# Working two weight chunks together in an fp32r matmul pipeline: all 512-column matmuls of both, then all 256-column matmuls of both

## What is computed

```python
for i in range(DEPTH):
    xn = rms_norm(h, norm_mix[i])
    mix = hgrn2_mixer(xn, ...) if i % 2 == 0 else short_conv_mixer(xn, ...)
    h = h + mix
    h = h + conv_glu_ffn(rms_norm(h, norm_ffn[i]), ffn_w_up[i], ffn_conv[i], ffn_w_down[i])
return rms_norm(h, final_norm)

# inside hgrn2_mixer
q, fr, v, g = jnp.split(xn @ w_in, ...)
f = lb + (1 - lb) * sigmoid(fr);  k = 1 - f
S_t = diag(f_t) S_{t-1} + k_t v_t^T;  o_t = S_t^T q_t      # per head
o = rms_norm(o, out_gain) * silu(g);  return o @ w_out
```

## Time and profile before

| | |
|---|---|
| median of 3 runs | 2368.76 us (2368.31 to 2370.46) |
| the profiled execution | 2369.03 us, of which the span of its instructions is 2367.2 us |
| PE busy | 2339.4 us, 99% |
| DVE busy | 1708.5 us, 72% |
| ACT busy | 1043.5 us, 44% |
| mean DMA rate | 184 GB/s |
| granted TensorE clock | 0.998 of full speed on average |

### The profile page before, as it was taken

One profiled execution on the slowest core, in us unless ns is written; L12 is line 12 of the kernel. 1 busy time (PEld: TensorE's weight loads), 2 busy tenths in 40 slices (PEclk: granted clock), 3 DMA queues, 4 the chain that ended last, 5 costly groups with the idle time before them and its releaser, 6 DMA issues.

```text
span 2367.2 us, 36548 instructions
## 1 busy us (share of the span) xinstructions
PE 2339.4 (99%) x13219; PEld 2049.0 (87%) x13219; DVE 1708.5 (72%) x2153; ACT 1043.5 (44%) x1151; POOL 2.7 (0%) x8
## 2 busy tenths in 40 slices
PE   7999999999999999999999999999999999999998
PEld 6888888888888888888888888888888888888886
DVE  6878788878878878865555666667788788785443
ACT  6443434454444444444444444444444444443443
POOL 0000000000000000000000000000000000000000
PEclk9999999999999999999999999999999999999999
DMA  6555555466666665655556656556656666665664
GB/s 197 169 179 160 166 160 164 152 192 188 186 194 185 187 194 179 194 190 187 188 185 192 188 187 187 187 188 186 194 180 192 189 184 188 193 202 185 193 193 144
DMA packets 411833, 434.90 MB, mean 184 GB/s; under 512 B 13344, under 2 KB 387040, under 8 KB 411616
## 3 DMA queue, kind: packets, MB, share of 16 engines
q1 hardware_dynamic: 411264, 432.51, 59.2%
q10 hardware_dynamic: 480, 1.18, 0.1%
HBM read 431.54 MB, written 2.10 MB: 183 GB/s over the span
## 4 chain that ended last, share of the span: by engine, by line
PE 96%; DVE 1%; issue 1%; ACT 1%; DMA 0%; SPq 0%; ACTq 0%; DVEq 0%
PE acc L1050 54%; PE acc L1056 28%; PE acc L1085 3%; PE acc L1086 3%; PE acc L1084 3%; PE acc L1068 2%; PE side L1179 1%; PE acc L1070 1%; PE side L1151 0%; DMA raw<-in_hgrn_w_in 0%; PE side L1174 0%; ACT w_parts L336 0%; DVE kl L788 0%; DVE a_diag L825 0%; DVE a_diag L819 0%
## 5 line engine op out<-in xcount | busy, mean ns | idle before, releaser
L545 DVE TENSOR_TENSOR w_parts<-raw,w_parts 128x1024 fp32r<-128x1024 f32 x816 | 994.4, 1223 | 578.9 <-ACT w_parts L336 569.0
L336 ACT ACTIVATE w_parts<-raw 128x1024 fp32r<-128x1024 f32 x816 | 862.6, 1060 | 1181.4 <-PE acc L1056 975.4
L1050 PE MATMUL acc<-xn,w_parts 128*128 128x512 f32 x4352 | 1094.5, 393 | 3.2 <-DVE xn L604 3.2
L1050 PEld LDWEIGHTS acc<-xn,w_parts 128*128 128x128 f32 x4352 | 783.7, 189 | 144.3 <-DVE xn L604 3.6
L1056 PEld LDWEIGHTS acc<-xn,w_parts 128*128 128x128 f32 x4352 | 594.1, 190 | 42.8
L1056 PE MATMUL acc<-xn,w_parts 128*128 128x256 f32 x4352 | 607.0, 282 | 0.0
L1050 PE MATMUL acc<-act,w_parts 128*128 128x512 f32 x1216 | 305.0, 393 | 1.6 <-DVE act L859 1.6
L1050 PEld LDWEIGHTS acc<-act,w_parts 128*128 128x128 f32 x1216 | 218.7, 189 | 41.0 <-DVE act L859 1.8
L1056 PEld LDWEIGHTS acc<-act,w_parts 128*128 128x128 f32 x1216 | 165.9, 190 | 11.9
L1056 PE MATMUL acc<-act,w_parts 128*128 128x256 f32 x1216 | 169.5, 282 | 0.0
L1084 PE MATMUL acc<-w_parts,act 128*128 128x512 f32 x352 | 137.3, 390 | 0.0
(11 more groups left out here) (131 smaller groups left out, 1005.2 us busy)
## 6 DMA issues: line engine op xcount, KB each, us to landing
raw<-in_ffn_w_up SPq DMA_DIRECT2D x352, 512.0 KB, 4.1
raw<-in_ffn_w_down SPq DMA_DIRECT2D x176, 512.0 KB, 4.3
raw<-in_hgrn_w_in SPq DMA_DIRECT2D x128, 512.0 KB, 3.6
raw<-in_sc_w_in SPq DMA_DIRECT2D x96, 512.0 KB, 4.5
raw<-in_hgrn_w_out SPq DMA_DIRECT2D x32, 512.0 KB, 3.6
raw<-in_sc_w_out SPq DMA_DIRECT2D x32, 512.0 KB, 4.6
x_tok<-in_x SPq DMA_DIRECT2D x4, 512.0 KB, 8.0
out<-h SPq DMA_DIRECT2D x4, 512.0 KB, 4.1
```

The source lines that it names most:

```text
L336: nc.scalar.activation(w_parts[:, c % RING, :, 0, :], raw[:, c % RING], ACT.Copy).then_inc(hi_ready, 1)
L545: v.tensor_tensor(w_parts[:, c % RING, :, 1, :], raw[:, c % RING], w_parts[:, c % RING, :, 0, :].bitcast(F32), ALU.subtract).then_inc(lo_r ...
L1050: mm(to[:, j, :], w[:, q, 0, j * P:(j + 1) * P], src[:, k * KW + q, :, :].rearrange("p n t -> p (n t)"), start=begin and q == 0, stop=Fals ...
```

## The change

The chunks are taken in pairs everywhere but in DOWN1. For a pair (k0, k0+1) TensorE does the 512-column matmuls of both chunks, then the `pieces` of chunk k0 (stages included), then the 256-column matmuls of both, then the pieces of k0+1. In the value group the 512-column matmuls read high and low weights (`token_boths`), the 256-column ones the high weights (`token_highs`). `chunk_used` is split in two semaphores: `hi_used` frees the high slot for ScalarE, `lo_used` the low slot for VectorE. For a feature chunk `hi_used` comes after its 512-column matmuls and `lo_used` after its 256-column ones; in the value group it is the other way round. In `PLAN`, level 0 moves from n = 3 to 4, level 2 from 6 to 7.

```diff
+RUN = 2
...
 LEVEL, OUTPUT = range(2)
-PLAN = [(2, LEVEL, -1), (3, LEVEL, 0), (5, LEVEL, 1), (6, LEVEL, 2), (8, LEVEL, 3), (10, LEVEL, 4),
+PLAN = [(2, LEVEL, -1), (4, LEVEL, 0), (5, LEVEL, 1), (7, LEVEL, 2), (8, LEVEL, 3), (10, LEVEL, 4),
         (12, LEVEL, 5), (13, LEVEL, 6), (15, LEVEL, 7), (18, OUTPUT, 0)]
...
-                act_e.wait_ge(chunk_used, at(i, phase.cpi, c + 1))
+                act_e.wait_ge(hi_used, at(i, phase.cpi, c + 1))
                 nc.scalar.activation(w_parts[:, c % RING, :, 0, :], raw[:, c % RING], ACT.Copy).then_inc(hi_ready, 1)
 
             def correction(i, phase, g, part, c):
 
-                act_e.wait_ge(chunk_used, at(i, phase.cpi, c + 1 + RING))
+                done = hi_used if phase is HGRN_IN and g == V_GROUP else lo_used
+                act_e.wait_ge(done, at(i, phase.cpi, c + 1 + RING))
                 a = g * phase.parts + part
                 act_e.wait_ge(acc_free, at(i, phase.api, phase.a0 + a + SETS))
...
                 dve.wait_ge(hi_ready, at(i, phase.cpi, c + 1))
+                dve.wait_ge(lo_used, at(i, phase.cpi, c + 1))
                 v.tensor_tensor(w_parts[:, c % RING, :, 1, :], raw[:, c % RING],
                                 w_parts[:, c % RING, :, 0, :].bitcast(F32), ALU.subtract).then_inc(lo_ready, 1)
...
-                        dve.wait_ge(chunk_used, at(i, phase.cpi, c + 1 + RING))
+                        dve.wait_ge(lo_used, at(i, phase.cpi, c + 1 + RING))
...
                 stage(s, [lambda to, j=j: mm(to[:, 0:T], ones[:], sq_acc[:, j, :], start=(j == 0), stop=(j == 1))
                           for j in range(2)] + (token_sums(T) if tokens_too else []))
 
-            def features(to, c, src, k, begin, end, await_low):
+            def feature_highs(to, c, src, k, begin):
 
                 w = w_parts[:, c % RING]
                 for q in range(KW):
                     for j in range(TW):
-
-                        mm(to[:, j, :], w[:, q, 0, j * P:(j + 1) * P],
-                           src[:, k * KW + q, :, :].rearrange("p n t -> p (n t)"), start=begin and q == 0, stop=False,
-                           skip_group_check=True)
-                await_low()
+                        o = mm(to[:, j, :], w[:, q, 0, j * P:(j + 1) * P],
+                               src[:, k * KW + q, :, :].rearrange("p n t -> p (n t)"), start=begin and q == 0,
+                               stop=False, skip_group_check=True)
+                o.then_inc(hi_used, 1)
+
+            def feature_lows(to, c, src, k, end):
+
+                w = w_parts[:, c % RING]
                 for q in range(KW):
                     for j in range(TW):
                         o = mm(to[:, j, T:], w[:, q, 1, j * P:(j + 1) * P], src[:, k * KW + q, 0, :], start=False,
                                stop=end and q == KW - 1, skip_group_check=True)
-                return o
-
-            def tokens(to, c, src, k, begin, end, await_low):
+                o.then_inc(lo_used, 1)
+
+            def x_block(src, t, n, b):
+
...
                 w = w_parts[:, c % RING]
-                await_low()
                 for q in range(KW):
-                    t = k * KW + q
                     for b in range(T // P):
-                        x_hi, x_lo = ((x_mirror[:, t, n] if b else src[:, t, n, 0:P]) for n in range(2))
-                        mm(to[:, b, :], x_hi, w[:, q].rearrange("p n d -> p (n d)"), start=begin and q == 0, stop=False,
-                           skip_group_check=True)
-                        o = mm(to[:, b, T:], x_lo, w[:, q, 0, :], start=False, stop=end and q == KW - 1,
-                               skip_group_check=True)
-                return o
-
-            def wide_tokens(to, c, src, k, begin, end, await_low):
+                        o = mm(to[:, b, :], x_block(src, k * KW + q, 0, b), w[:, q].rearrange("p n d -> p (n d)"),
+                               start=begin and q == 0, stop=False, skip_group_check=True)
+                o.then_inc(lo_used, 1)
+
+            def token_highs(to, c, src, k, end):
 
                 w = w_parts[:, c % RING]
-                await_low()
+                for q in range(KW):
+                    for b in range(T // P):
...
-                        o = mm(bank, x_lo, hi, start=False, stop=end and q == KC - 1)
-                return o
+                        low = mm(bank, x_hi, lo, start=False, stop=False)
+                        high = mm(bank, x_lo, hi, start=False, stop=end and q == KC - 1)
+                low.then_inc(lo_used, 1)
+                high.then_inc(hi_used, 1)
 
             def phase_of(phase, src, ready, ready0, per=1, rs=None, pieces=None, carry=None, rs_at=(0, RS_AT)):
+
+                def between(i, first, g, kk):
+                    if carry and first:
+                        carry(g, kk)
+                    if first and rs and (g, kk) == rs_at:
+                        sum_squares(*rs)
+                    if pieces:
+                        pieces(i, first, g, kk)
...
-                            pe.wait_ge(hi_ready, at(i, phase.cpi, c + 1))
-                            work = features
-                            if first and phase is HGRN_IN and g == V_GROUP and part == 0:
-                                pe.wait_ge(mirror_ready, k + 1)
+                        steps = phase.steps(first, g)
+                        run = 1 if phase is DOWN1 else RUN
+                        for k0 in range(0, phase.cpg, run):
+                            chunks = []
+                            for kk in range(k0, k0 + run):
+                                part, k, begin, end = steps[kk]
+                                c = phase.c0 + g * phase.cpg + kk
+                                a = g * phase.parts + part
+                                if begin:
+
+                                    pe.wait_ge(acc_free, at(i, phase.api, phase.a0 + a + 1))
+                                need = k + 1 if phase.parts == 2 else k * KC // TG + 1
+                                if first and g == 0 and need > seen:
+                                    pe.wait_ge(ready, ready0 + need * per)
+                                    seen = need
+                                pe.wait_ge(hi_ready, at(i, phase.cpi, c + 1))
+                                to = acc[:, a % SETS]
+                                if phase is DOWN1:
+                                    pe.wait_ge(lo_ready, at(i, phase.cpi, c + 1 + RING))
+                                    wide_tokens(to, c, src, k, begin, end)
+                                elif phase is HGRN_IN and g == V_GROUP:
+                                    if first and part == 0:
+                                        pe.wait_ge(mirror_ready, k + 1)
+                                    pe.wait_ge(lo_ready, at(i, phase.cpi, c + 1 + RING))
+                                    token_boths(to, c, src, k, begin)
+                                else:
+                                    feature_highs(to, c, src, k, begin)
+                                chunks.append((c, to, k, end))
                             if phase is DOWN1:
-                                work = wide_tokens
-                            elif phase is HGRN_IN and g == V_GROUP:
-                                work = tokens
-                            work(acc[:, a % SETS], c, src, k, begin, end, await_low).then_inc(chunk_used, 1)
-                            if carry and first:
-                                carry(g, kk)
-                            if first and rs and (g, kk) == rs_at:
-                                sum_squares(*rs)
-                            if pieces:
-                                pieces(i, first, g, kk)
+                                between(i, first, g, k0)
+                                continue
+                            for kk in range(k0, k0 + run - 1):
+                                between(i, first, g, kk)
+                            for c, to, k, end in chunks:
+                                if phase is HGRN_IN and g == V_GROUP:
+                                    token_highs(to, c, src, k, end)
+                                else:
+                                    pe.wait_ge(lo_ready, at(i, phase.cpi, c + 1 + RING))
+                                    feature_lows(to, c, src, k, end)
+                            between(i, first, g, k0 + run - 1)
                 loop(pe, phase, body)
 
-            pe.sem_inc(chunk_used, RING)
+            pe.sem_inc(hi_used, RING)
```

More of the change, by code:

```diff
@@ L207, in trunk @@
         lo_ready = sem("lo_ready")
-        chunk_used = sem("chunk_used")
+        hi_used = sem("hi_used")
+        lo_used = sem("lo_used")
         acc_free = sem("acc_free")
@@ L475, in final @@
                 if first and (g, kk) == (0, 0):
-                    act_e.wait_ge(chunk_used, DOWN1.c0 + RING)
+                    act_e.wait_ge(lo_used, DOWN1.c0 + RING)
```

(40 more changed lines are left out.)

7 lines of the change are left out of this document (added).

## The result

| | before | after |
|---|---|---|
| median of 4 runs beside each other | 2369.59 us (2368.31 to 2370.46) | 2385.99 us (2385.4 to 2388.3) |
| ratio, with its 95% interval | | 1.007 (1.0057 to 1.0082) |
| span of the profiled execution | 2367.2 us | 2383.6 us |
| granted clock, mean | 0.998 | 0.994 |

The change costs 16.4 us, in the median and in the span alike. The forecast was +8.7 with its top at 2386: the direction is right, the size is about half of what came.

What follows compares the result with a forecast made beforehand. TensorE, busy 99% of the span, was taken as the bound, so any new wait is paid in full. Terms -7.3 + 10.0 + 4.2 + 1.8 = +8.7 on 2369.03 gave 2378 us; own range 2373.5 to 2383, full range 2366 to 2386.

Steps and rivals of the forecast that it cites:

- Change 1: Feature and value-group pairs: one switch per pair instead of per chunk saves 0.020 us in each of 364 pairs, -7.3 us.
- Change 2: HGRN_IN level stages: TensorE waits 2.1 us at stage 1 and 0.9 us over stages 3 to 6, +10.0 us.
- Change 3: Start of HGRN_OUT: last activation tiles come 3.3 us later and more work stands behind them, +4.2 us.
- Change 4: Start-up: activation times stay, but 4.7 us of work instead of 3.0 stands behind the wait ending at 29.16, +1.8 us.
- waits smaller: Rival: VectorE gets through n = 2 and 3 faster, level stages cost what they do now, 2367.7 us; chance 0.18.
- faster: Rival: each saved switch is worth more, 2360 us at 0.07 a pair, or the waits are away, 2361; chance 0.14.
- No saving per pair: Rival: the switch's cost grows with the run, or the skill's rule holds, 2385 us; chance 0.10.
- More waits: Rival: levels 3 and 4 also wait between a pair's runs, 1 us more in each iteration, 2382 us; chance 0.08.

Runs made afterwards that it cites:

- the version with the longer wait: Three unused VectorE multiplications added ahead of level 1's operands in each iteration, against the kernel before, without pairs: 2385.17 us, ratio 1.0063.
- another version, with the same waits: The changed kernel with HGRN_OUT alone put back to chunk by chunk: 2379.0 us, ratio 1.004 against the kernel before.

## Why the prediction was right and where it was wrong

**Change 1 (-7.3) was right.** 0.020 us a pair in 284 pairs measured by themselves, and the whole of it is seen in the version that has pairs only there. The formula of the Trainium skill (TensorE: Matmul & The Clock Gate, section "Back-to-back issue gap"), which the page calls that of isolated matmuls, has no term for what came before, so by it the pairs would gain nothing. The measured 2.779, 2.7835 and 2.793 us a chunk with quads, pairs and single chunks decide against it.

**Change 2 (+10.0) was right in its waits and lacked a term.** In the third iteration, where the clock stayed, everything stands where the working put it. Times after P0 = 281.92: level 1's stage begins at +21.56 (forecast 21.5), after 2.0 us (2.1); the later stages come 1.2 us later than without waits (0.9), of which 0.9 are idle time in the timeline. VectorE's rows, beside the earlier trace rows:

```profile
295.17 1.23 DVE L549 TENSOR_TENSOR w_parts<-raw,w_parts 128x1024 fp32r<-128x1024 f32 x1 [3.58 <-ACT w_parts L338]
298.14 1.21 DVE L549 TENSOR_TENSOR w_parts<-raw,w_parts 128x1024 fp32r<-128x1024 f32 x1
301.27 0.68 DVE L809 TENSOR_TENSOR fpre<-fpre 128x512 f32<-128x512 f32 x1
302.60 0.76 DVE L792 TENSOR_TENSOR kl<-kh,suf 128x256 f32<-128x256 f32 x2
```

The split of n = 2 starts at +13.25 (forecast 13.25), that of n = 3 at +16.22 (16.21), the operands end at +21.44 (21.4). The iteration is 2.44 us longer; forecast were 2.5 of waits less 0.3 of pairs. The other three iterations pay 1.6 us more each for a granted clock of 0.5. This is the step that failed: the working took a wait to cost its own length and 0.1 of refill, and priced no slower work behind it.

**Change 3 (+4.2) failed in the same way.** The tiles came within 0.15 us of the forecast, and TensorE then did the next run at half speed, 1.7 us more.

**Change 4 (+1.8) was right.** The first iteration is 5.59 longer; less 2.44 and the 1.6 of its level 1 that leaves 1.6. (The forecast's own terms, 1.9 + 0.8 + 1.9 less 3.0, add up to 1.6 too, not to 1.8.) The clock was low in the start-up too, as the forecast allowed:

```profile
19.24 3.22 PE L1053 MATMUL acc<-xn,w_parts 128*128 128x512 f32 x8 [2.28 <-DVE xn L608]
22.25 1.57 PE L1033 MATMUL side<-ident,x_tok 128*128 128x128 f32 x8
...
28.75 2.12 PE L1053 MATMUL acc<-xn,w_parts 128*128 128x512 f32 x8 [1.18 <-DVE xn L608]
```

The run from 19.24 took 3.0 us instead of 1.84, and the wait that ends at 28.75 hid it. There the question was asked, "should the clock rise later because TensorE idles", and answered by cover. It wasn't asked of the waits at level 1 and in HGRN_OUT, which are about as long or longer and have no cover behind them.

The sum, then: +8.7 as forecast, four stretches of the lower clock at 1.6 make +6.4, in all 15.1 of 16.4. Of the remaining 1.3 us about 1.0 are in the level stages, whose delay was 0.2 to 0.3 us an iteration longer than forecast, and the rest in HGRN_OUT.

Of the rivals, "waits smaller" is refuted by the list of waits, and "faster" by it and by the 0.020 us a pair. "No saving per pair" gives 2385 us, within 1 us of the measured time, and is refuted as well, by the pace in UP0: a right total for a wrong reason. "More waits" holds in a small part (0.3 us an iteration, not 1).

The Trainium skill (TensorE: Matmul & The Clock Gate, section "HAM oscillation — how this bites in real kernels") says that TensorE falls back to the lower clock when its wait between bursts of matmuls is long enough, and that the next burst then starts slow. The traces here agree with that: 3 of 4 level 1 waits of 2.0 us in the changed kernel, the one of 5.8 us, and 4 of 4 waits of 3.15 us in the version with the longer wait were followed by 0.50. No wait up to 1.7 us was, 22 of which are from 1.3 us up.

But a wait of 2 to 3 us is not followed by it each time, and the kernel before shows that itself: behind the 2.76 us that end at 29.16 the clock stayed at 1.00. Of the 13 waits of 2.00 to 2.95 us on activations in the start-up of the twelve traces, eight have a stretch at 0.50 beside or behind them and five have none. The windows view behind that wait in the kernel before, in the version with pairs only from UP0 on (2.70 us), and in the one that has the new `PLAN` besides (2.95 us); all three have the same order of matmuls here:

```profile
29.16:32.50 3.34, 3.34 (x19) 2.81 (x19) 3.16 (x4) 3.31 (x7) 0.00 (x0) 1.00 0.26 68
...
29.37:32.76 3.39, 3.39 (x10) 2.65 (x9) 3.13 (x4) 3.36 (x7) 0.00 (x0) 0.50 0.36 103
...
28.81:32.20 3.39, 3.39 (x19) 2.86 (x20) 3.13 (x4) 3.36 (x7) 0.00 (x0) 1.00 0.32 72
```

The first iteration takes 110.74 us in the second of them and 109.35 in the third. For such a wait a forecast can give a price and a chance, not a fixed cost.

## What to carry to other kernels

Price a new wait of TensorE at its length plus what the slower clock behind it takes from the next work: here 1.6 us behind 11 of 12 level 1 waits of 2.0 to 3.2 us, nothing behind waits up to 1.7 us. By these prices two short waits are cheaper than one long one of the same sum (twelve waits with 5.1 us cost 0.4 us each and no clock), so when stages move, spread the delay; no two versions here have the same sum, so this is worked out, not measured. And group work by kind only in the phases without a stage between, and only as far as the ring of slots leaves room: two chunks at a time in a ring of four gained 5.7 us, four at a time lost 30. When an engine waits, go back along its program to the last wait ahead of the instruction that released it; the largest sum in the list of waits can be another one.

## What was not expected of the hardware

- The granted clock fell to 0.5 behind a single wait of 2.0 us, and stayed there for 3.4 us of full work, in 3 of 4 cases; the fourth, with the same wait to 0.01 us, kept 1.00. In another version, with the same waits, it fell in 4 of 4. What decides between them isn't settled.
- The fall doesn't come at a fixed point: at once with the first matmul behind a wait of 2.0 us, 1.1 us later in the fourth iteration of the same kernel, behind the same wait (409.03 against 407.93), 1.2 us later behind one of 3.15 us (199.50 against 198.31). In HGRN_OUT it came inside the wait: TensorE stood idle from 461.02, the clock fell at 463.66, and work came back at 466.83.
- Of the four executions of the version with the longer wait, two list a mean granted clock of 0.999 and two of 0.995 and 0.996. The first are only 1.7 us faster (2384.1 and 2384.5 against 2385.8 and 2386.3), where four stretches less would be 6 us. Only one execution, of the second kind, has a trace, so what the others did instead is open.
- What it costs to come from 256-column matmuls to 512-column ones, some 0.03 us, doesn't grow with the run: by the times per chunk above it is the same after 8, 16 and 32 matmuls.
